# A two-layer decoder step with routed experts: the order of the shared expert's blocks, the count and the first gather

## The chip, the cores and the metric

The kernel runs on one core of a Trainium2 chip. A core has a matrix engine (PE, TensorE), a vector engine (DVE), a scalar engine (ACT), a general engine (POOL), and SP, which here only issues transfers. All transfers run on 16 DMA engines. Each engine works through its own instructions in order, and they meet only at semaphores. The metric is the device time of one execution in microseconds, lower is better.

## The reference

320 tokens (256 of a prompt, 8 x 8 of samples) of width 1024 pass two layers in float32. Layer 0 mixes tokens by sliding-window attention, layer 1 by gated linear attention. Each is followed by a mixture of experts, which is the part that the change touches:

```python
scores = sigmoid(x @ router_w); sel = scores + router_b
# 4 of 8 groups by their two best scores, then the 8 best experts of 64 for each token
w = w / sum(w) * 2.5
routed[t] = sum over the 8 experts e of t:  w[t, e] * (silu(x_t @ wg[e]) * (x_t @ wu[e])) @ wd[e]
shared    = (silu(x @ swg) * (x @ swu)) @ swd
out       = routed + shared          # SHARED_FF = EXPERT_FF = 256
```

Each of the 64 experts has 3 MB of weights in a layer (three matrices of 1024 x 256), and all of them are read, so that the two layers read some 400 MB for the experts alone.

## The kernel before, in words

`moe(l)` has a head, in which the experts are sorted by how many tokens chose them, and then 29 passes. Rank 0 is the expert with the most tokens, and every rank has a fixed number of slots (96, 64 or 32; what doesn't fit is done by `rest` behind the passes). A pass (`PASSES`) does two or three ranks at a time, 128 slots in all: pass 0 the ranks 0 and 56, pass 1 the ranks 1 and 57, pass 2 three ranks. Up to four passes make a batch (`BATCHES` = 2, 4, 4, ...), whose tokens are gathered together.

Weights come through two rings. `gu_ring` has five slots of 2 MB for gate and up weights, `dn_ring` five of 1 MB for down weights. SP issues the gate and up weights of all experts in the order of the passes (`expert_stream`), and those of down for the first five; it begins when the order is known (`order_full`), and ahead of each expert it waits until PE is through with the slot (`last_item`). ACT issues the other down weights. Two of the five slots of `gu_ring` first hold the shared expert's weights: gate and up in one, down in the other. They are given free by `item_used.up(pe.drain())`, once behind the shared expert's last block of gate and up, once behind the shared down product; the fourth and the fifth expert go into them.

The head, on PE: router logits; transposes of the tokens into rows (`token_rows`); the shared expert's gate and up products in four blocks `shared_up(f, u, ks)` of eight chunks `ks` each, with the steps of the sorting set between them. These steps are the count (how many tokens chose each expert, ten small bf16 matmuls from L1615 to L1626, which need the top-8 mask of DVE, `topk_full`, and the rows copied by ACT, `tok_hi`), the sort (L1629 and L1630, a permutation matrix that DVE forms from the count), the transposes of the weights (L1634) and the positions (L1640). DVE (from L1669) forms mask, permutation, order, weights, positions and parts of weights in turn; it also forms the shared expert's hidden values, a product with what ACT's SiLU gives (`ovh`, `sh_h`). POOL forms the low halves of the token rows (`tok_lo`) once the order is known.

Then, in the second block of code, on PE: the shared down product (L1842) into the banks that sum the output; `fill(0, f)` for f = 0 to 3 (L1808), which gathers the tokens of the first batch by matmuls with the selection `sel` that DVE forms (`select(0)`, L1990), while ACT (L1922) and DVE (L1998) copy the gathered tokens out; `slot_weights(0)` (L1818), the weight of each slot, which ACT copies out and forms (L1927 to L1935). After that the passes: gate and up (L1869), the gather for the next batch, transposes (L1890), the scatter of the pass before (`combine`, L1830 and L1833), down (L1908).

Of the kernel before, what the change touches and what calls it, by code (L numbers as in the profile page):

```python
# [24 lines left out]
ALU = mybir.AluOpType  # L25
# [5 lines left out]
KC = D // P  # L31
# [3 lines left out]
T = SEQ + NS  # L35
# [26 lines left out]
def places(experts):  # L62

    out, o = [], 0
    for r, cap in experts:
        out.append((r, cap, o))
        o += cap
    return out
# [18 lines left out]
NB = len(BATCHES)  # L87
NFILL = 4 + 8 * (NB - 1)
# [143 lines left out]
def decoder_step(nc, a, debug=None):  # L232
    with ExitStack() as ctx:
        names = {}

        def sb(name, shape, dt=F32, c=ctx):
            names[name] = names.get(name, -1) + 1
            return c.enter_context(nc.sbuf_tensor(f"s_{name}_{names[name]}", shape, dt))

        def sem(name):  # L240
            return ctx.enter_context(nc.semaphore(name))
# [5 lines left out]
        bank = [pair[i // 2][:, i % 2, :] for i in range(4)]  # L247
# [21 lines left out]
        def cc(name):  # L269
            at, n = lay[name]  # L270
            part = next(p for p, (lo, hi) in const_range.items() if lo <= at < hi)
            lo = const_range[part][0]
            return csts[part][:, at - lo:at - lo + n]
# [1189 lines left out]
        S = {n: sem(n) for n in SEMS}  # L1463
# [55 lines left out]
        def moe(l):  # L1519
            with ExitStack() as c:  # L1520
# [8 lines left out]
                ovh = sb("ovh", [P, 2, T], c=c)  # L1529
# [4 lines left out]
                def step(ins):  # L1534
                    settled(nc.vector, ins)

                with ExitStack() as c1:
# [30 lines left out]
                    def _(pe):  # L1568
# [32 lines left out]
                        def shared_up(f, u, ks):  # L1601

                            for k in ks:
                                last = pe.matmul(bank[2 + 2 * f + u][:, 0:T], shw[:, k, FF * u + P * f:FF * u + P * f + P], hT[:, k, :],  # L1604
                                                 start=(k == 0), stop=(k == KC - 1))
                            return last

                        slot_in[sg_].wait(pe, sg_n)
                        shared_up(0, 0, range(KC))
                        pe.wait_ge(S["tok_hi"], 6 * l + 6)  # L1610
                        pe.wait_ge(S["topk_full"], l + 1)
                        pe.wait_ge(A["mod_full"], mod_at(19 + 4 * l))
# [11 lines left out]
                        pe.matmul(W1[:, 128:192], ones_b, m0, start=True, stop=False)  # L1624
                        pe.matmul(W1[:, 128:192], ones_b, m1, start=False, stop=False)
                        pe.matmul(W1[:, 128:192], up2[0:NS, :], m2, start=False, stop=True).then_inc(S["cnt_psum"], 1)  # L1626
                        shared_up(0, 1, range(0, 2))
                        pe.wait_ge(S["perm_full"], l + 1)
                        pe.matmul(W0[0:1, 384:448], cc("ecol")[0:NE, :], perm[0:NE, :], start=True, stop=True)  # L1629
                        pe.matmul(W0[0:1, 448:512], cols[0:NE, 2:3], perm[0:NE, :], start=True, stop=True).then_inc(S["sort_psum"], 1)  # L1630
                        shared_up(0, 1, range(2, KC)).then_inc(S["sh_psum"], 1)
                        pe.wait_ge(S["pw_full"], l + 1)
                        for t in range(3):
                            last = pe.transpose(W1[:, t * P:(t + 1) * P], pw[:, t, :, :].rearrange("p u e -> p (u e)"), ident)  # L1634
# [34 lines left out]
                    def _(dve):  # L1669
# [63 lines left out]
                        step(dve.tensor_tensor(wovS[:, :, :], posS[:, :, :], cc("caprow").unsqueeze(1).to_broadcast([P, 3, NE]), ALU.subtract))  # L1733
                        step(dve.tensor_scalar(wovS[:, :, :], wovS[:, :, :], -BIG, None, ALU.is_ge))
                        step(dve.tensor_tensor(wovS[:, :, :], wovS[:, :, :], w_, ALU.mult))
                        dve.wait_ge(S["sh_silu"], 2 * l + 2)
                        dve.tensor_tensor(ovh[:, 1, :], ovh[:, 1, :], bank[5][:, 0:T], ALU.mult).then_inc(S["sh_h"], 1)

                c2 = ExitStack()
                sel = sb("sel", [P, 3, 4 * P], F32R, c=c2)  # L1740
# [59 lines left out]
                def _(pe):  # L1800
                    def fill(q, f):

                        b = (W1, W2)[f % 2]
                        width = P * BATCHES[q]
                        ms = (2 * f, 2 * f + 1) if q == 0 else (f,)
                        for x, m in enumerate(ms):
                            for n, (w, s) in enumerate(shown):
                                last = pe.matmul(b[:, width * x:width * x + width], w[:, m * P:(m + 1) * P], sel[:, s, 0:width],  # L1808
                                                 start=(n == 0), stop=(n == 4))
                        last.then_inc(S["fill_full"], 1)  # L1810

                    def slot_weights(q):

                        for j in range(BATCHES[q]):
                            ranks = [r for r, _ in PASSES[BATCH_START[q] + j]]
                            n4, at = 4 * len(ranks), 256 + 16 * j
                            for s in range(3):
                                last = pe.matmul(W0[:, at:at + n4].rearrange("p (e u) -> p e u", u=4), sel[:, s, P * j:P * j + P],  # L1818
                                                 wpartS[:, s, ranks[0]:ranks[-1] + 1:ranks[1] - ranks[0], :], start=(s == 0), stop=(s == 2))
                        return last  # L1820

                    def combine(p):
# [11 lines left out]
                                                 stop=(p == NP - 1 and y is ylo and half == 1))  # L1834
                        return last

                    slot_in[sd_].wait(pe, sd_n)
                    pe.wait_ge(S["sh_h"], 2 * (l + 1))
                    for t, (t0, tn) in enumerate(TILES):
# [2 lines left out]
                                last = pe.matmul(acc[(t, half)], ovh[:, f, t0:t0 + tn], shd[:, f, 512 * half:512 * half + 512],  # L1842
                                                 start=(f == 0), stop=False)
                    item_used.up(pe.drain())
                    pe.wait_ge(S["tok_lo"], 3 * (l + 1))
                    for f in range(4):
                        pe.wait_ge(S["sel_full"], l * NB + 1)
                        if f >= 2:
                            pe.wait_ge(S[("fill_act", "fill_dve")[f % 2]], l * NFILL // 2 + 1)
                        fill(0, f)  # L1850
                    slot_weights(0).then_inc(S["tr_full"], 1)

                    for p in range(NP):
                        if p == NP - 1:
# [3 lines left out]
                        if j == 0:  # L1858
                            f = 3 if q == 0 else 7
# [116 lines left out]
                @block.vector  # L1976
                def _(dve):
                    def select(q):

                        for h in range(BATCHES[q]):  # L1980
                            experts = PASSES[BATCH_START[q] + h]
                            caps = [cap for _, cap in experts]
                            if len(set(caps)) == 1:
                                n, cap, r0 = len(experts), caps[0], experts[0][0]
                                last = dve.tensor_tensor(sel[:, :, h * P:(h + 1) * P].rearrange("p t (e s) -> p t e s", s=cap),
                                                         cc("slot")[:, 0:cap].unsqueeze(1).unsqueeze(1).to_broadcast([P, 3, n, cap]),
                                                         posS[:, :, r0:r0 + n].unsqueeze(3).to_broadcast([P, 3, n, cap]), ALU.is_equal)
                            else:
                                for r, cap, o in places(experts):
                                    last = dve.tensor_tensor(sel[:, :, h * P + o:h * P + o + cap],  # L1990
                                                             cc("slot")[:, 0:cap].unsqueeze(1).to_broadcast([P, 3, cap]),
                                                             posS[:, :, r:r + 1].to_broadcast([P, 3, cap]), ALU.is_equal)
                        last.then_inc(S["sel_full"], 1)

                    def fill_out(q, f):

                        dve.wait_ge(S["fill_full"], filled(q, f))
                        dve.tensor_copy(fill_target(q, f), fill_source(q, f)).then_inc(S["fill_dve"], 1)  # L1998

                    dve.wait_ge(S["tok_lo"], 3 * (l + 1))  # L2000
                    select(0)
                    dve.wait_ge(S["h_kept"], 16 * (l + 1))
                    fill_out(0, 1)
                    fill_out(0, 3)
                    dve.wait_ge(S["tr_full"], l * (NP + 1) + 1)
                    select(1)
                    for p in range(NP):
                        if p == NP - 1:
                            left = any_left(dve)
                        q = BATCH_OF[p][0]  # L2010
                        dve.wait_ge(S["silu_full"], l * NP + p + 1)
                        dve.wait_ge(S["hT_full"], hT_at(p))
                        dve.scalar_tensor_tensor(hh[:, :], sg[:, :], wsl[p % 2][:, 0:1], W0[:, FF:2 * FF], ALU.mult, ALU.mult).then_inc(S["hh_full"], 1)  # L2013
                        for f in fills_in(p)[1::2]:
                            fill_out(q + 1, f)
                        for half in range(2):
                            dve.wait_ge(S["y_high"], 2 * (l * NP + p) + half + 1)
                            dve.tensor_tensor(ylo[:, half, :], (W1, W2)[half], yhi[:, half, :].bitcast(F32), ALU.subtract).then_inc(S["y_low"], 1)  # L2018
                            if half == 0:
                                dve.tensor_scalar(gt[:, :], cc("token"), wsl[p % 2][:, 1:2], None, ALU.is_equal).then_inc(S["gt_full"], 1)  # L2020
                        if last_of(p) and q + 2 < NB:
                            select(q + 2)
                    rest_dve(dve, left)
# [306 lines left out]
```

## Time and profile before

| | |
|---|---|
| median of 3 runs | 1546.19 us (1544.91 to 1547.66) |
| the profiled execution | 1550.64 us, its span 1548.5 us |
| mean granted TensorE clock | 0.979 |
| PE busy | 1461.7 us, 94% |
| DVE, ACT busy | 27%, 25% |
| DMA | 509.64 MB, mean 329 GB/s |

The profile is of one execution; times in it count from the start of its span. A busy share is an average over stages with different limits. Ends of matmuls are modelled. The chain of waits is the work that ended last, followed back from step to step; a stretch that it names "issue" is time in which the engine waited for nothing that the profile shows. The experts of layer 0 run from about 280 to 758 us, those of layer 1 from about 1040 to 1521 us.

### The profile page before, as it was taken

Reading aid. Unit: us, or ns where it says so; the run is one execution under the profiler, and the core shown is the slowest. Engines: PE = TensorE matmul, PEld = TensorE weight load, DVE = VectorE, ACT = ScalarE, POOL = GpSimd, SP = SyncE. Lnnn points to the kernel's source line nnn. Section 1 sums busy time; section 2 is a strip of 40 time slices with the busy share of each in tenths; the row PEclk is TensorE's granted clock in tenths of the full one; section 3 lists DMA queues with packets and bytes.
Section 4 is the critical chain, followed back from the end, with each engine's and each line's share of the span. In section 5 each row is a group of like instructions: output and inputs, shape, how many; then the busy total and the mean of one; then the engine's idle time right before and its main releaser. Section 6 shows DMA issues by size and latency. Waiting matters only on the chain.

```text
span 1548.5 us, 21530 instructions
## 1 busy us (share of the span) xinstructions
PE 1461.7 (94%) x8438; PEld 745.5 (48%) x8438; DVE 411.5 (27%) x998; ACT 383.4 (25%) x1089; POOL 49.9 (3%) x86
## 2 busy tenths in 40 slices
PE   6998999999999999999999989999999999999896
PEld 2344655544444444544465445554444544545444
DVE  2126524222121212211353142432121221211113
ACT  3024313222221212211363122412222221221113
POOL 0000301000000000000100010010000000000000
PEclk9998999999999999999999998999999999999998
DMA  9987506999999999999851252198999999999981
GB/s 395 395 326 287 201 28 249 395 361 421 420 421 420 421 421 422 420 420 421 330 218 55 109 204 91 53 371 336 407 420 420 421 421 421 422 421 421 411 335 35
DMA packets 65894, 509.64 MB, mean 329 GB/s; under 512 B 7776, under 2 KB 8048, under 8 KB 10208
## 3 DMA queue, kind: packets, MB, share of 16 engines
q1 hardware_dynamic: 45072, 366.43, 57.5%
q10 hardware_dynamic: 16992, 123.74, 19.4%
q0 software_dynamic: 3728, 18.07, 3.2%
q8 instruction: 69, 1.13, 0.3%
q14 instruction: 33, 0.27, 0.0%
HBM read 499.16 MB, written 11.01 MB: 329 GB/s over the span
## 4 chain that ended last, share of the span: by engine, by line
PE 79%; DMA 13%; ACT 3%; DVE 2%; issue 1%; SPq 1%; ACTq 0%; DVEq 0%
PE bank L1869 24%; PE banks L1908 11%; DMA s_gu_ring<-in_moe_wu_dram 10%; PE banks L1808 7%; PE banks L431 5%; PE banks L1066 4%; PE ybank L1830 3%; PE banks L1830 3%; PE bank L1833 3%; PE banks L679 2%; PE bank L498 2%; PE banks L1094 2%; DMA s_gu_ring<-in_wqkv_dram 2%; DMA s_gu_ring<-in_ada_w_dram 2%; PE banks L1604 1%
## 5 line engine op out<-in xcount | busy, mean ns | idle before, releaser
L1869 PE MATMUL bank<-s_gu_ring,s_hbuf 128*32 128x512 f32 (+1 forms) x2752 | 415.0, 602 | 18.1 <-DMA s_gu_ring<-in_moe_wu_dram 14.1
L1869 PEld LDWEIGHTS bank<-s_gu_ring,s_hbuf 128*32 128x32 f32 (+1 forms) x2752 | 130.2, 121 | 293.7 <-issue 293.7
L1908 PE MATMUL banks<-s_dn_ring,s_hTs 128*32 128x512 f32 (+1 forms) x1376 | 211.5, 596 | 7.1 <-ACT s_hTs L1958 5.2
L2018 DVE TENSOR_TENSOR s_ylo<-banks,s_yhi 128x512 fp32r<-128x512 f32 x116 | 80.2, 691 | 328.9 <-ACT s_yhi L1966 328.9
L1808 PE MATMUL banks<-s_sel,s_htok 128*128 128x512 f32 (+2 forms) x640 | 149.4, 381 | 0.5 <-issue 0.5
L1808 PEld LDWEIGHTS banks<-s_sel,s_htok 128*128 128x128 f32 x640 | 109.8, 188 | 61.6 <-issue 45.2
L1966 ACT CAST s_yhi<-banks 128x512 fp32r<-128x512 f32 x116 | 67.9, 586 | 268.8 <-PE banks L1908 268.8
L2013 DVE SCALAR_TENSOR_TENSOR s_hh<-s_sg,s_wsl,bank 128x256 f32<-128x256 f32 x58 | 27.9, 480 | 348.4 <-ACT s_sg L1950 348.4
L1908 PEld LDWEIGHTS banks<-s_dn_ring,s_hTs 128*32 128x32 f32 (+1 forms) x1376 | 58.4, 119 | 128.1 <-issue 120.9
L1950 ACT ACTIVATE s_sg<-bank 128x256 f32<-128x256 f32 x58 | 22.3, 384 | 389.2 <-PE bank L1869 389.2
L1998 DVE COPY s_hbuf<-banks 128x512 f32<-128x512 f32 (+1 forms) x60 | 40.4, 673 | 119.0 <-PE banks L1808 119.0
L1066 PE MATMUL banks<-s_gu_ring,s_hbuf 128*128 128x512 f32 x128 | 55.9, 593 | 0.5 <-DVE s_rs L1350 0.5
L1922 ACT COPY s_hbuf<-banks 128x512 f32<-128x512 f32 (+1 forms) x60 | 34.3, 572 | 80.7 <-PE banks L1808 80.7
L1934 ACT ACTIVATE s_wsl<-s_rstd 32x1 f32<-32x1 f32 (+1 forms) x172 | 50.2, 292 | 3.0
L679 PE MATMUL banks<-s_gu_ring,s_hbuf 128*128 128x512 f32 x96 | 44.4, 617 | 3.4 <-DMA s_gu_ring<-in_wqkv_dram 3.4
L1830 PE MATMUL ybank<-s_yhi,s_gt 128*128 128x512 f32 x116 | 41.3, 437 | 0.0
L431 PE MATMUL banks<-s_qk,s_gu_ring 128*128 128x320 f32 x128 | 38.0, 461 | 0.8 <-ACT s_qk L1287 0.8
L1066 PEld LDWEIGHTS banks<-s_gu_ring,s_hbuf 128*128 128x128 f32 x128 | 24.2, 191 | 29.1 <-issue 28.2
L431 PE MATMUL banks<-s_hbuf,s_gu_ring 128*128 128x320 f32 x128 | 36.8, 450 | 0.9 <-DVE s_hbuf L974 0.9
L1830 PE MATMUL banks<-s_yhi,s_gt 128*128 128x512 f32 x116 | 36.3, 394 | 0.0
L1830 PE MATMUL ybank<-s_ylo,s_gt 128*128 128x512 f32 x116 | 36.1, 392 | 0.0
L1830 PE MATMUL banks<-s_ylo,s_gt 128*128 128x512 f32 x116 | 36.0, 392 | 0.0
(409 smaller groups left out, 1489.6 us busy)
## 6 DMA issues: line engine op xcount, KB each, us to landing
s_gu_ring<-in_moe_wg_dram SPq DMA_DIRECT2D x128, 1024.0 KB, 14.6
s_gu_ring<-in_moe_wu_dram SPq DMA_DIRECT2D x128, 1024.0 KB, 19.9
s_dn_ring<-in_moe_wd_dram ACTq DMA_DIRECT2D x118, 1024.0 KB, 12.8
s_gu_ring<-in_ada_w_dram SPq DMA_DIRECT2D x24, 2048.0 KB, 12.2
s_gu_ring<-in_win_dram SPq DMA_DIRECT2D x6, 2048.0 KB, 12.1
s_dn_ring<-in_moe_wd_dram SPq DMA_DIRECT2D x10, 1024.0 KB, 17.1
s_gu_ring<-in_wqkv_dram SPq DMA_DIRECT2D x3, 2048.0 KB, 25.6
s_gu_ring<-in_wo_dram SPq DMA_DIRECT2D x2, 2048.0 KB, 8.4
```

The costliest lines, as they stand in the source:

```text
L431: last = pe.matmul(b[:, 0:T], item(slot)[:, k, (m % 4) * P:(m % 4 + 1) * P], src[:, k, :], start=(k == 0), stop=(k == KC - 1))
L679: last = pe.matmul(b[:, :], hT[:, k, t0:t0 + P], item(slots[cch])[:, k, :], start=(k == 0), stop=(k == KC - 1))
L1066: last = pe.matmul(b[:, :], hT[:, k, t0:t0 + P], w[:, k, :], start=(k == 0), stop=(k == KC - 1))
L1808: last = pe.matmul(b[:, width * x:width * x + width], w[:, m * P:(m + 1) * P], sel[:, s, 0:width], start=(n == 0), stop=(n == 4))
L1830: pe.matmul(acc[(t, half)], g[:, t * P:(t + 1) * P], y[:, half, :], start=False, stop=(p == NP - 1 and y is ylo))
L1833: last = pe.matmul(bank[6][:, :], g[:, 320 - 64 * half:448 - 64 * half], y[:, half, :], start=False, stop=(p == NP - 1 and y is ylo and ha ...
L1869: last = pe.matmul(W0[o:o + n, :], tokens_of(p, k)[:, o:o + n], w[:, k, :, :], start=(k == 0), stop=(k == KC - 1))
L1908: last = pe.matmul((W1, W2)[half][o:o + n, :], hTs[:, f, o:o + n], dn_ring[:, dn_of[(l, r)][0], w0:w0 + 512], start=(f == 0), stop=(f == 1))
L1934: act.activation(wsl[p % 2][o:o + n, 0:1], w[:, 0:1], ACT.Identity, bias=w[:, 1:2])
L1966: act.copy(yhi[:, half, :], (W1, W2)[half]).then_inc(S["y_high"], 1)
L1998: dve.tensor_copy(fill_target(q, f), fill_source(q, f)).then_inc(S["fill_dve"], 1)
L2018: dve.tensor_tensor(ylo[:, half, :], (W1, W2)[half], yhi[:, half, :].bitcast(F32), ALU.subtract).then_inc(S["y_low"], 1)
```

## The change

Two things are put in another order, and nothing is added or left out. In the head, the first block of the shared expert is cut: its chunks 0 to 3 stay ahead of the count, 4 and 5 come between count and sort, 6 and 7 and the whole second block behind the sort (before: the whole first block ahead of the count, two chunks of the second between, six behind). In the second part, the gather for the first batch and its slot weights come ahead of the shared down product that frees the slot. On DVE the product of the shared expert's second half moves from the end of the first part to behind the first selection.

```diff
--- before.py
+++ after.py
@@ -1606,7 +1606,7 @@
                             return last
 
                         slot_in[sg_].wait(pe, sg_n)
-                        shared_up(0, 0, range(KC))
+                        shared_up(0, 0, range(4))
                         pe.wait_ge(S["tok_hi"], 6 * l + 6)
                         pe.wait_ge(S["topk_full"], l + 1)
                         pe.wait_ge(A["mod_full"], mod_at(19 + 4 * l))
@@ -1624,11 +1624,12 @@
                         pe.matmul(W1[:, 128:192], ones_b, m0, start=True, stop=False)
                         pe.matmul(W1[:, 128:192], ones_b, m1, start=False, stop=False)
                         pe.matmul(W1[:, 128:192], up2[0:NS, :], m2, start=False, stop=True).then_inc(S["cnt_psum"], 1)
-                        shared_up(0, 1, range(0, 2))
+                        shared_up(0, 0, range(4, 6))
                         pe.wait_ge(S["perm_full"], l + 1)
                         pe.matmul(W0[0:1, 384:448], cc("ecol")[0:NE, :], perm[0:NE, :], start=True, stop=True)
                         pe.matmul(W0[0:1, 448:512], cols[0:NE, 2:3], perm[0:NE, :], start=True, stop=True).then_inc(S["sort_psum"], 1)
-                        shared_up(0, 1, range(2, KC)).then_inc(S["sh_psum"], 1)
+                        shared_up(0, 0, range(6, KC))
+                        shared_up(0, 1, range(KC)).then_inc(S["sh_psum"], 1)
                         pe.wait_ge(S["pw_full"], l + 1)
                         for t in range(3):
                             last = pe.transpose(W1[:, t * P:(t + 1) * P], pw[:, t, :, :].rearrange("p u e -> p (u e)"), ident)
@@ -1733,8 +1734,6 @@
                         step(dve.tensor_tensor(wovS[:, :, :], posS[:, :, :], cc("caprow").unsqueeze(1).to_broadcast([P, 3, NE]), ALU.subtract))
                         step(dve.tensor_scalar(wovS[:, :, :], wovS[:, :, :], -BIG, None, ALU.is_ge))
                         step(dve.tensor_tensor(wovS[:, :, :], wovS[:, :, :], w_, ALU.mult))
-                        dve.wait_ge(S["sh_silu"], 2 * l + 2)
-                        dve.tensor_tensor(ovh[:, 1, :], ovh[:, 1, :], bank[5][:, 0:T], ALU.mult).then_inc(S["sh_h"], 1)
 
                 c2 = ExitStack()
                 sel = sb("sel", [P, 3, 4 * P], F32R, c=c2)
@@ -1834,6 +1833,13 @@
                                                  stop=(p == NP - 1 and y is ylo and half == 1))
                         return last
 
+                    pe.wait_ge(S["tok_lo"], 3 * (l + 1))
+                    for f in range(4):
+                        pe.wait_ge(S["sel_full"], l * NB + 1)
+                        if f >= 2:
+                            pe.wait_ge(S[("fill_act", "fill_dve")[f % 2]], l * NFILL // 2 + 1)
+                        fill(0, f)
+                    slot_weights(0).then_inc(S["tr_full"], 1)
                     slot_in[sd_].wait(pe, sd_n)
                     pe.wait_ge(S["sh_h"], 2 * (l + 1))
                     for t, (t0, tn) in enumerate(TILES):
@@ -1842,13 +1848,6 @@
                                 last = pe.matmul(acc[(t, half)], ovh[:, f, t0:t0 + tn], shd[:, f, 512 * half:512 * half + 512],
                                                  start=(f == 0), stop=False)
                     item_used.up(pe.drain())
-                    pe.wait_ge(S["tok_lo"], 3 * (l + 1))
-                    for f in range(4):
-                        pe.wait_ge(S["sel_full"], l * NB + 1)
-                        if f >= 2:
-                            pe.wait_ge(S[("fill_act", "fill_dve")[f % 2]], l * NFILL // 2 + 1)
-                        fill(0, f)
-                    slot_weights(0).then_inc(S["tr_full"], 1)
 
                     for p in range(NP):
                         if p == NP - 1:
@@ -1999,6 +1998,8 @@
 
                     dve.wait_ge(S["tok_lo"], 3 * (l + 1))
                     select(0)
+                    dve.wait_ge(S["sh_silu"], 2 * l + 2)
+                    dve.tensor_tensor(ovh[:, 1, :], ovh[:, 1, :], bank[5][:, 0:T], ALU.mult).then_inc(S["sh_h"], 1)
                     dve.wait_ge(S["h_kept"], 16 * (l + 1))
                     fill_out(0, 1)
                     fill_out(0, 3)
```

## Rows read from the trace of the kernel before

**Rows 1.** The page: busy time; DMA by slice of 38.7 us; the chain's lines.

```profile
PE 1461.7 (94%) x8438; PEld 745.5 (48%) x8438; DVE 411.5 (27%) x998; ACT 383.4 (25%) x1089; POOL 49.9 (3%) x86
...
DMA  9987506999999999999851252198999999999981
...
PE bank L1869 24%; PE banks L1908 11%; DMA s_gu_ring<-in_moe_wu_dram 10%; PE banks L1808 7%; PE banks L431 5%; PE banks L1066 4%; PE ybank L1830 3%; PE banks L1830 3%; PE bank L1833 3%; PE banks L679 2%; PE bank L498 2%; PE banks L1094 2%; DMA s_gu_ring<-in_wqkv_dram 2%; DMA s_gu_ring<-in_ada_w_dram 2%; PE banks L1604 1%
```

**Rows 2.** Busy by stretch: stretch, length, each engine, PEclk, DMA share, GB/s.

```profile
340.00:355.00 15.00, 15.00 (x116) 7.18 (x116) 2.91 (x5) 4.00 (x13) 0.00 (x0) 1.00 1.01 423
```

**Rows 3.** Instructions in time, PE: start, length, what, [idle before <- what ended it].

```profile
681.94 8.41 PE L1869 MATMUL bank<-s_gu_ring,s_hbuf 128*32 128x512 f32 x64 [3.29 <-DMA s_gu_ring<-in_moe_wu_dram]
...
1443.52 9.91 PE L1869 MATMUL bank<-s_gu_ring,s_hbuf 128*32 128x512 f32 x64 [4.33 <-DMA s_gu_ring<-in_moe_wu_dram]
```

**Rows 4.** Busy by stretch, first transfers and behind the second pass.

```profile
250.00:252.50 2.50, 2.50 (x13) 1.73 (x12) 2.24 (x5) 0.43 (x2) 2.50 (x2) 1.00 0.63 187
...
315.00:317.00 2.00, 2.00 (x25) 0.69 (x20) 0.46 (x1) 0.59 (x1) 0.00 (x0) 1.00 0.49 205
317.00:319.00 2.00, 2.00 (x24) 0.73 (x20) 1.34 (x4) 0.58 (x1) 0.00 (x0) 1.00 0.08 29
```

**Rows 5.** Chain of waits, layer 0, 230 to 300 us: start, length, what.

```profile
241.90 4.31 PE banks L1604 x16
...
247.02 1.27 PE banks L1604 x4
...
257.49 4.52 PE ybank L1604 x16
...
263.21 3.67 PE ybank L1842 x8
266.88 3.43 PE banks L1842 x8
270.31 1.87 PE bank L1842 x8
...
272.44 5.05 PE banks L1808 x40
...
280.04 7.07 PE bank L1869 x64
```

**Rows 6.** Instructions in time, layer 0, what the steps of the head need.

```profile
242.45 0.65 ACT L1660 CAST s_htok<-banks 64x512 fp32r<-64x512 f32 x1
...
242.77 0.63 DVE L1697 TENSOR_TENSOR s_mb<-s_mm,s_slc 128x192 bf16<-128x192 f32 x2
...
254.22 2.34 POOL L1563 TENSOR_TENSOR s_htok<-s_hbuf,s_htok 64x1024 fp32r<-64x1024 f32 x1 [0.50 <-POOL s_htok L1563]
...
260.29 0.35 DVE L1735 TENSOR_TENSOR s_wovS<-s_wovS,banks 128x192 f32<-128x192 f32 x1
...
262.03 0.44 ACT L1666 ACTIVATE s_ovh<-ybank 128x320 f32<-128x320 f32 x1 [9.15 <-PE ybank L1604]
...
262.98 1.16 DVE L1990 TENSOR_TENSOR s_sel<-s_cst,s_posS 128x288 fp32r<-128x288 f32 x4
...
277.31 0.73 PE L1818 MATMUL bank<-s_wpartS,s_sel 128*128 128x8 f32 x6
...
279.65 0.17 ACT L1935 COPY s_wsl<-s_rstd 32x1 f32<-32x1 f32 x1
```

**Rows 7.** Layer 1: slot weights in time; the first pass in the chain.

```profile
1037.29 0.73 PE L1818 MATMUL bank<-s_wpartS,s_sel 128*128 128x8 f32 x6
...
1040.01 8.58 PE bank L1869 x64
```

**Rows 8.** Issues of SP in time: the first and the fifth expert's gate weights.

```profile
249.83 0.35 SPq L1496 DMA_DIRECT2D s_gu_ring<-in_moe_wg_dram  x1
...
272.80 0.35 SPq L1496 DMA_DIRECT2D s_gu_ring<-in_moe_wg_dram  x1
```

**Rows 9.** Busy by stretch, layer 1, start of the first pass.

```profile
1040.00:1042.50 2.50, 2.49 (x12) 0.67 (x16) 0.39 (x2) 0.00 (x0) 0.00 (x0) 0.50 0.98 403
```

## Prediction

> **What bounds the kernel now.** I read the page's shares first, then the busy time by stretches, then the chain of waits around the routing and the head of the experts, then the instructions in order of time there. The page shows TensorE (PE) busy for 94% of the span and the DMA slices at 9 for nearly all of both expert stages [rows 1]. Two resources are thus close to their limit, and the question is which of them sets the time of an expert stage, and from where on. By stretches [rows 2] the 16 DMA engines move some 421 GB/s from 340 us on (the row shown is the first of 27 of 15 us up to 745, of which none is under 416), and transfers of gate and up weights hold 10% of the chain [rows 1]; the last of them in each layer end PE's waits at 681.94 and 1443.52 us, and from there PE runs to the end of the layer without them [rows 3]. Before that, however, the engines stand nearly still: their share is 0.49 and 0.08 between 315 and 319 us [rows 4]. In that hole nothing is queued; it ends when PE has finished work and so freed buffers. So every transfer after the hole goes out at a time that PE sets, and the late transfers are requests of the same uninterrupted queue. I conclude that the head of the experts, up to the third pass, is PE's, and that whatever PE gains there moves the rest of the layer, transfers included, by the same amount.
>
> In the head the chain [rows 5] is PE without a gap from 241.90 to 262.01 us: first shared block, count, the second block in two pieces, transposes, the other two blocks. Then come two holes. PE waits 1.20 us (262.01 to 263.21) for SiLU and the product on DVE, before the shared down product. And after the gather (to 277.49) and the slot weights, first pass at 280.04: the slot weights start at 277.31 and last 0.73, so PE stands from 278.04 to 280.04, 2.00 us, for ACT, which copies the weights out and forms the slots, last at 279.65 + 0.17 [rows 6]. The second layer repeats the pattern: its second hole runs from 1037.29 + 0.73 = 1038.02 to 1040.01 [rows 7].
>
> **Part 1, half a block of the shared expert ahead of the count.** Four of the eight chunks of a block now follow the count instead of preceding it. A block of eight takes 4.31 us [rows 5], so the count can start 2.15 us earlier, at 244.06. What it waits for is ready: the top-8 mask ends at 242.77 + 0.63 = 243.40, the last rounded token row at 242.45 + 0.65 = 243.10 [rows 6]; 0.6 us is left. DVE's permutation and the sort follow with the same two chunks between, also 2.15 us earlier, and with them the order of the experts, the DMA issues of SP and POOL's subtractions. PE itself gains nothing: the same chunks are only in another order, the number of switches is the same, and there was no idle time to remove between 241.90 and 262.01. Between sort and transposes ten chunks stand now instead of six, so PE comes there at the same time as before, while DVE's weights move forward with the count. Cost on the path: 0. What moves is the first expert's transfer: issue 249.83 becomes 247.68 [rows 8]. The share of 0.63 in 250.0 to 252.5 [rows 4] puts the first data at 250.93, 1.1 us after the issue; it becomes 248.78. But the first pass needs only two experts, and 3 x 1.049 MB at 423 GB/s [rows 2] are 7.44 us for one: they are there by 265.8 before, 263.7 after, and are wanted at 277. Gain bounded by 0 and 2.15 us a layer (the whole advance, were the transfers the bound); I take 0.
>
> **Part 2, gather and slot weights ahead of the shared down product.** It uses both holes. After 262.01 PE needs the first selection. On DVE this now comes ahead of the shared product: it starts where that began to wait, at 260.29 + 0.35 = 260.64, takes 1.16 and is ready at 261.8 [rows 6]. POOL's last subtraction ended at 254.22 + 2.34 = 256.56 [rows 6] and comes 2.15 us earlier. So PE goes on after a drain; the same drain cost 0.26 ahead of the gather (270.31 + 1.87 = 272.18 to 272.44) [rows 5]. Then: 262.01 + 0.26 + gather 5.05 + slot weights 0.55 (277.49 to 278.04) = 267.87; shared down 3.67 + 3.43 + 1.87 = 8.97 = 276.84; drain 0.25 = 277.09 for the first pass, against 280.04. **2.95 us a layer.** What covers the moved waits: ACT's slots (1.8 us after the slot weights) and the last DVE copy lie beside 8.97 us of shared down, with 7 us to spare. DVE's shared product waits for the SiLU, which ends at 262.03 + 0.44 = 262.47 [rows 6]; 0.5 us later it is done, and is wanted at 267.9. Queued behind it on DVE are the gather's copies, the first of them wanted 2.5 us after the gather starts, at 264.8, so they lose nothing. ACT has its SiLU ahead of its first copy, which is wanted at 263.5. Within the gather the third and fourth block wait for copies of the first two as before, and stood for nothing there. Should the selection or the block edge be late, the cost is bounded by the old hole of 1.20 us; should the drain turn out free, 0.26 is gained. I take 2.95, with 2.0 and 3.2 as ends (3.2 is the sum of both holes).
>
> **The slot that comes free later.** The buffer of the shared down weights is freed by the drain behind that product, and the fifth expert goes into it. SP issued it at 272.80, 0.62 after PE's end at 272.18 [rows 5, 8]. Now it is 276.84 + 0.62 = 277.5, 4.7 us later, with first data 1.1 us after that, 278.6. Four experts last until 248.78 + 4 x 7.44 = 278.54. So the engines pause by 0.1 us at most, and the fifth expert is complete at 286.0 (288.1 before). Next is the sixth, issued after the first pass: 277.09 + 7.07 + 0.2 = 284.4, ahead of that. The third pass, which uses the fifth expert, starts at 314.6. Cost: 0. The Trainium skill ("DMA: Bandwidth & Descriptors", Anatomy of one DMA) gives about 2.0 us of fixed cost for one DMA; by that figure the pause would be near 1 us and still ends before PE has use for the data. The trace's issue-to-data of 1.1 us is shorter, since it leaves out the completion.
>
> **The clock.** In layer 1 the granted clock falls to 0.50 (1.2 GHz) in 1040.0 to 1042.5, right behind the hole of 2.00 us and the tiny slot-weight matmuls [rows 9], and the first pass takes 8.58 us instead of 7.07 [rows 5, 7]. In layer 0 the same hole costs nothing: 7.07. So the hole's removal is worth 0 or 1.51 us a layer beyond its length. The Trainium skill ("TensorE: Matmul & The Clock Gate", What's actually happening) says that the slow state is the default and activity lifts it; by that rule the dense shared down ahead of the first pass keeps the clock up. Since the timed runs lie 4.45 us below the profiled one, I can't tell how often they pay this; I take 0.3 us for both layers, ends 0 and 3.0.
>
> **The sum.** Two layers x 2.95 = 5.9. Against the profiled execution, 1550.64 us (span 1548.5 and 2.1 around it), with its own slow first pass gone: 1550.64 - 5.9 - 1.5 = 1543.2. The median of the runs is 1546.19: 1546.19 - 5.9 - 0.3 = **1540.0 us**. Ends by the terms: 1546.19 - 4.0 = 1542.2 and 1546.19 - 6.4 - 3.0 = 1536.8.
>
> **Rivals.** (1) The stream is the bound from its start. For it: the DMA slices at 9 right behind the start [rows 1]. Then a layer gains what the fifth expert gains, 2.1 us: 1542.0. Against it: the hole at 315 to 319.
>
> (2) The gain is swallowed by the late waits. PE waited 3.29 and 4.33 us for transfers at 681.94 and 1443.52 [rows 3]; if the stream doesn't move, these grow by 2.95 and nothing is left: 1546.2. For it: their 10% of the chain; against it the same hole.
>
> (3) Slower: as (2), and the longer waits cost the clock. After those two waits the first pass took 8.41 and 9.91 us instead of 7.07, and behind them the layer is PE's to its end, so this is paid. A pass wholly at 1.2 GHz takes 14.1: at most 5.7 + 4.2 = 9.9 us, half of it as an estimate, 5.0: 1551.2. It decides as soon as the stream moves by less than PE; if both move together the waits keep their length, which speaks against it.
>
> **Chances.** Forecast 0.78, (1) 0.08, (2) 0.09, (3) 0.05. A measurement of this kernel can tell 0.2%, 3.1 us, from no change, so faster means below 1543.1: 0.82 (the forecast but for 0.01 of it, and most of (1)); same 0.13; slower 0.05. The forecast's own range is 1537 to 1543; to hold 8 in 10 with the clock's share on either side I give 1536.5 to 1544.
>
> **What would show it.** Right: count at 244.1 with no wait ahead of it; PE going from the last shared block into the gather within 0.3 us; first pass some 3 us earlier in relation to the first shared block, at clock 1.0; the hole in the transfers still there behind the second pass; late waits of PE as long as before; both layers shorter by 3 us. Wrong: PE waiting ahead of the gather for the selection, a stall within it, the hole gone, or late waits longer by what the head gained. The forecast falls if the time is above 1543.1.

## The result and the profile after

| | before | after |
|---|---|---|
| median of 5 runs | 1546.19 us (1544.91 to 1551.18) | 1539.40 us (1537.76 to 1541.54) |
| profiled execution, span | 1550.64, 1548.5 us | 1539.78, 1537.8 us |
| mean granted TensorE clock | 0.979 | 0.981 |

The medians lie 6.8 us apart. The ratio of the two kernels' runs is 0.9949, 7.9 us less, with an interval of 0.9932 to 0.9967, that is 5.1 to 10.5 us less. Forecast were 1540.0 us, in 1536.5 to 1544.

The page of the changed kernel, the lines that answer to [rows 1]:

```profile
PE 1456.9 (95%) x8438; PEld 744.6 (48%) x8438; DVE 411.8 (27%) x998; ACT 383.3 (25%) x1089; POOL 49.7 (3%) x86
...
DMA  9987506999999999999851252198999999999981
...
PE bank L1868 24%; PE banks L1907 11%; DMA s_gu_ring<-in_moe_wu_dram 8%; PE banks L1807 8%; PE banks L431 5%; PE banks L1066 4%; PE ybank L1829 3%; PE banks L1829 3%; PE bank L1832 3%; PE banks L679 2%; PE banks L1094 2%; DMA s_gu_ring<-in_ada_w_dram 2%; PE bank L498 2%; DMA s_gu_ring<-in_wqkv_dram 1%; PE banks L1604 1%
```

Such a page hardly shows a change of 0.5%: the shares are nearly those of before, and the slices of the transfers are the same digit for digit. The chain of waits in the head of layer 0 does (start, length, what), and answers to [rows 5]. Line numbers behind the change differ by one to six: the gather is L1807, the slot weights L1817, the shared down product L1848, gate and up of a pass L1868.

```profile
240.18 2.15 PE banks L1604 x8
242.33 0.03 PE bank L1615
...
244.73 5.58 PE banks L1604 x20
...
259.15 1.18 DVE s_sel L1989 x4
260.32 0.21 issue
260.53 5.03 PE banks L1807 x40
265.56 0.57 PE bank L1817 x6
266.13 3.54 PE ybank L1848 x8
269.67 3.43 PE banks L1848 x8
273.10 1.88 PE bank L1848 x8
274.97 0.36 issue
275.34 7.07 PE bank L1868 x64
```

The first shared block is cut in two without a wait at the count. The selection is ready at 260.33 (259.15 + 1.18), the gather starts at 260.53, and nothing but 0.36 us behind the drain lies between the last of the shared down product and the first pass. From the first shared block to the first pass it is 275.34 - 240.18 = 35.16 us; before it was 280.04 - 241.90 = 38.14 [rows 5]. **The head is 2.98 us shorter, where 2.95 were forecast**, and in layer 1 it is the same: 1031.91 - 996.76 = 35.15, against 38.13. In that layer the first pass takes 7.07 us again, where before it took 8.58 [rows 7].

Beyond the head the spans of the two executions add up so: -1.72 us ahead of layer 0's head, -2.98 head, +0.36 passes of layer 0, -0.78 between the layers, -2.98 head, -2.60 from the first pass of layer 1 to the end; together -10.7. The parts other than the heads are of a size that differs from one execution to the next: in the run of part 1 alone, below, layer 0's head too begins 1.74 us earlier than in the kernel before (240.00 against 241.74), and nothing ahead of it was touched. The passes' own share is mostly the clock: of the +0.36, 0.33 is the slow pass behind layer 0's last wait for transfers (8.74 against 8.41), and of the -2.60, 1.51 is the first pass of layer 1 and 1.14 the pass behind its last wait (8.77 against 9.91). Hence the median, which moved by 6.8, is nearer to the two heads (5.96) than the span of the profiled pair is.

The late waits of PE, the last for transfers in each layer, are as long as before. In time order, the passes that answer to [rows 3]:

```profile
677.27 8.74 PE L1868 MATMUL bank<-s_gu_ring,s_hbuf 128*32 128x512 f32 x64 [2.99 <-DMA s_gu_ring<-in_moe_wu_dram]
...
1433.96 8.77 PE L1868 MATMUL bank<-s_gu_ring,s_hbuf 128*32 128x512 f32 x64 [4.29 <-DMA s_gu_ring<-in_moe_wu_dram]
```

2.99 and 4.29 us against 3.29 and 4.33: had the transfers stayed where they were, these would be 6.3 and 7.3. The transfers moved with PE's head. From the start of the first pass of layer 0 to the end of this wait it is 401.90 us before (681.94 - 280.04) and 401.93 after (677.27 - 275.34). In layer 1 it is 403.51 and 402.05; the 1.5 more before are the slow first pass, which came through in full.

### The profile page after: what moved, and what is told of

The parts are those of the page before. It is cut to its first block, busy times and chain, and to the rows that moved or that the text cites. A ratio compares the mean times of both kernels' runs of the same rounds, so it can differ in the third digit from the quotient of the medians.

```text
span 1537.8 us, 21530 instructions
## 1 busy us (share of the span) xinstructions
PE 1456.9 (95%) x8438; PEld 744.6 (48%) x8438; DVE 411.8 (27%) x998; ACT 383.3 (25%) x1089; POOL 49.7 (3%) x86
## 4 chain that ended last, share of the span: by engine, by line
PE 81%; DMA 11%; DVE 3%; ACT 3%; issue 1%; SPq 1%; ACTq 0%; DVEq 0%
PE bank L1868 24%; PE banks L1907 11%; DMA s_gu_ring<-in_moe_wu_dram 8%; PE banks L1807 8%; PE banks L431 5%; PE banks L1066 4%; PE ybank L1829 3%; PE banks L1829 3%; PE bank L1832 3%; PE banks L679 2%; PE banks L1094 2%; DMA s_gu_ring<-in_ada_w_dram 2%; PE bank L498 2%; DMA s_gu_ring<-in_wqkv_dram 1%; PE banks L1604 1%
## 5 line engine op out<-in xcount | busy, mean ns | idle before, releaser
L1868 PE MATMUL bank<-s_gu_ring,s_hbuf 128*32 128x512 f32 (+1 forms) x2752 | 414.3, 601 | 13.3 <-DMA s_gu_ring<-in_moe_wu_dram 12.6
L1868 PEld LDWEIGHTS bank<-s_gu_ring,s_hbuf 128*32 128x32 f32 (+1 forms) x2752 | 130.1, 120 | 289.9 <-issue 289.9
L1807 PE MATMUL banks<-s_sel,s_htok 128*128 128x512 f32 (+2 forms) x640 | 149.3, 381 | 0.5 <-DVE s_sel L1989 0.5
L1807 PEld LDWEIGHTS banks<-s_sel,s_htok 128*128 128x128 f32 x640 | 109.8, 188 | 60.8 <-issue 44.4
L1949 ACT ACTIVATE s_sg<-bank 128x256 f32<-128x256 f32 x58 | 22.3, 384 | 401.4 <-PE bank L1868 401.4
```

What stands on the lines that cost most here:

```text
L1868: last = pe.matmul(W0[o:o + n, :], tokens_of(p, k)[:, o:o + n], w[:, k, :, :], start=(k == 0), stop=(k == KC - 1))
```

## The experiments

The experiments ran in three sets, each on another chip: e1 to e4, e5 to e8, e9 to e12. Runs of the kernel before had a median of 1546.19 us in the first, 1545.63 in the second and 1545.82 in the third. Of these, only the first has the changed kernel (e3). So differences against it are taken from the ratios to the kernel before, with e3 as the changed kernel's (0.9954), times 1546. "Head" is the time from the first matmul of the first shared block to the first of the first pass (38.3 us before, 35.3 after, by the instructions in order of time).

**e1, the first part alone.** The kernel before with

```diff
-                        shared_up(0, 0, range(KC))
+                        shared_up(0, 0, range(4))
...
-                        shared_up(0, 1, range(0, 2))
+                        shared_up(0, 0, range(4, 6))
...
-                        shared_up(0, 1, range(2, KC)).then_inc(S["sh_psum"], 1)
+                        shared_up(0, 0, range(6, KC))
+                        shared_up(0, 1, range(KC)).then_inc(S["sh_psum"], 1)
```

> Only the first part of the change: four chunks of the first shared block ahead of the count instead of eight. Theory (PE sets the head, the start of the transfers has slack): issue of the first expert 2.1 us earlier after the first shared block, first pass as late as before (38.1 us after the first shared block), time of before within 1 us, ratio 0.999 to 1.001. Rival (the stream is the bound from its start): 2.1 us less a layer, 1542, ratio 0.997.

Measured: 1547.22 us, ratio 1.0005 (0.9992 to 1.0019); heads 38.30 and 38.28 us, and both first passes slow, 8.52 and 8.77 us. The start of the transfers moves as it should. In the order of time:

```profile
240.00 2.32 PE L1604 MATMUL banks<-s_hbuf,s_gu_ring 128*128 128x320 f32 x8
...
245.94 0.35 SPq L1496 DMA_DIRECT2D s_gu_ring<-in_moe_wg_dram  x1
```

That is 5.94 us from the shared block to the first issue, against 8.09 before (241.74 to 249.83 [rows 8]): 2.15 us earlier, and worth nothing. The rival's ratio of 0.997 is outside the interval.

**e2, the second part alone.** The changed kernel with the three edits of e1 taken back.

> Only the second part: gather and slot weights ahead of the shared down product, and the product on DVE behind the first selection; the count as before. Theory: the whole gain, first pass 35.15 us after the first shared block, 1540, ratio 0.995 to 0.996. Rival (the parts help only together, since the fifth expert's transfer goes out 3 us later and needs the earlier start): a part of the 3 us a layer comes back as longer late waits, 1543 or more.

Measured: 1540.01 us, ratio 0.9960 (0.9946 to 0.9975); heads 35.33 and 35.33. The whole gain of the heads is here; the 0.9 us that the ratio of e3 is lower are within both intervals. The late waits were 4.24 and 4.02 us, no longer than the 4.29 us of the changed kernel; the parts don't need each other.

**e3, the changed kernel again.** No edit.

> The changed kernel once more, as the measure for this set: 1539.4 us, ratio 0.995. With the first result it says how far two measurements of one kernel lie apart.

Measured: 1538.95 us, ratio 0.9954 (0.9938 to 0.9970). Two measurements of one kernel lie 0.45 us apart.

**e4, the transfers start 3 us later.** The changed kernel with

```diff
                 sp.wait_ge(S["order_full"], l + 1)
+                sp.wait_ge(S["pw_full"], l + 1)
```

> The changed kernel, but SP starts the experts' transfers only when the token weights are formed as well, which is 2.9 us later than the order. Theory: the transfers pause for 4 us and more behind the second pass anyway, so the later start is taken from that pause and the time stays at that of the changed kernel (within 1 us); late waits of PE as long as before. Rival (the stream is the bound): 2.9 us more a layer, 1545.

Measured: 1540.04 us, ratio 0.9958 (0.9946 to 0.9971): 0.6 us above e3, with intervals that cover each other; heads 35.32 and 35.36. The first issue comes 8.91 us behind the start of the shared block (5.95 in the changed kernel), so 3.0 us later. The rival's 1545 us, a ratio of 0.9992, is outside. Busy time by stretch shows where the 3 us went. First the changed kernel, then e4 (stretch, length, engines, PEclk, DMA share, GB/s):

```profile
300.00:305.00 5.00, 5.00 (x31) 4.36 (x30) 0.82 (x2) 1.82 (x5) 0.00 (x0) 1.00 0.91 331
305.00:310.00 5.00, 4.02 (x23) 2.71 (x25) 0.69 (x1) 1.33 (x8) 0.00 (x0) 1.00 1.00 419
310.00:315.00 5.00, 5.00 (x52) 1.89 (x48) 2.47 (x7) 1.17 (x2) 0.00 (x0) 1.00 0.54 180
```

```profile
300.00:305.00 5.00, 5.00 (x31) 4.38 (x30) 0.69 (x1) 2.00 (x6) 0.00 (x0) 1.00 1.01 423
305.00:310.00 5.00, 4.06 (x26) 2.66 (x28) 0.69 (x1) 1.15 (x7) 0.00 (x0) 1.00 1.01 421
310.00:315.00 5.00, 5.00 (x52) 1.80 (x48) 2.69 (x8) 1.17 (x2) 0.00 (x0) 1.00 0.74 267
```

The pause behind the second pass is shorter (0.54 became 0.74, and 0.91 became 1.01); the later start was taken from it. Summed over the stretches of 5 us from 295 to 335, the bytes fall short of a steady 423 GB/s by 6.9 us in the changed kernel and by 3.9 us in e4.

**e5, 11 us later.** The same line with `S["sort_psum"], 2 * l + 2`.

> The changed kernel, but SP starts the experts' transfers only when the positions are summed, some 10.8 us later than the order. Theory: the first pass still finds its two experts (landed by 273, wanted at 275); the pause of the stream behind the second pass, worth between 3.8 us by its share and 7 us by its bytes, is used up, and the rest, 4 to 7 us a layer, comes out as longer late waits: 1547 to 1553. Rival (PE's head alone sets the time, transfers never): 1539.4. Rival (the stream is the bound from its start): 10.8 us a layer, 1561.

Measured: 1546.91 us, ratio 1.0008 (0.9997 to 1.0019), 8.3 us above the changed kernel: 4.2 a layer, of 10.8 that the start was delayed. Both rivals, 1539.4 and 1561, are outside. The heads are still 35.33 and 35.31. The pause is gone (the same stretches as above, of e5):

```profile
300.00:305.00 5.00, 5.00 (x32) 3.80 (x24) 1.17 (x2) 1.55 (x3) 0.00 (x0) 1.00 1.00 413
305.00:310.00 5.00, 4.77 (x24) 3.72 (x24) 0.20 (x1) 1.98 (x10) 0.00 (x0) 1.00 1.02 426
310.00:315.00 5.00, 4.29 (x40) 1.47 (x44) 1.55 (x3) 1.17 (x2) 0.00 (x0) 1.00 1.02 423
```

From the first pass to the last late wait's end it is now 405.6 us in layer 0 (682.39 - 276.81) and 405.5 in layer 1, where it was 401.9 and 402.1. In one thing the expectation was off: the last waits are not longer (2.76 and 2.95 us). The loss comes as new, earlier waits, this one among them:

```profile
381.45 7.07 PE L1869 MATMUL bank<-s_gu_ring,s_hbuf 128*32 128x512 f32 x64 [2.01 <-DMA s_gu_ring<-in_moe_wu_dram]
```

So the start of the transfers has a slack between 3 and 11 us; 10.8 - 4.2 = 6.6 a layer, if what is beyond the slack comes through in full. It agrees with the 6.9 us that the pause was worth by its bytes.

**e6, the product ahead of the selection.** The changed kernel with DVE's order as before:

```diff
+                    dve.wait_ge(S["sh_silu"], 2 * l + 2)
+                    dve.tensor_tensor(ovh[:, 1, :], ovh[:, 1, :], bank[5][:, 0:T], ALU.mult).then_inc(S["sh_h"], 1)
                     dve.wait_ge(S["tok_lo"], 3 * (l + 1))
                     select(0)
-                    dve.wait_ge(S["sh_silu"], 2 * l + 2)
-                    dve.tensor_tensor(ovh[:, 1, :], ovh[:, 1, :], bank[5][:, 0:T], ALU.mult).then_inc(S["sh_h"], 1)
```

> The changed kernel, but DVE forms the shared expert's product ahead of the first selection, as before the change. Theory: PE then waits for the selection, which comes after SiLU (0.5), product (0.5) and selection (1.2): the gather starts 2.3 us after the last shared block instead of 0.2, so 2.1 us more a layer, 1543.6. Rival (the gather's place alone carries the gain): 1539.4.

Measured: 1545.30 us, ratio 0.9998 (0.9987 to 1.0009). The whole gain is gone, 6.8 us above the changed kernel, where 4.2 were expected. The instructions of the head in layer 0:

```profile
262.19 0.49 DVE L2000 TENSOR_TENSOR s_ovh<-s_ovh,ybank 128x320 f32<-128x320 f32 x1 [1.86 <-ACT s_ovh L1667]
...
262.59 1.16 DVE L1989 TENSOR_TENSOR s_sel<-s_cst,s_posS 128x288 fp32r<-128x288 f32 x4
...
263.89 6.52 PE L1807 MATMUL banks<-s_sel,s_htok 128*128 128x256 f32 x40 [2.21 <-DVE s_sel L1989]
```

The wait is 2.21 us, about as worked out. But the gather behind it takes 6.52 us instead of 5.03, and the stretch says why (PEclk, the granted clock, is the third number from the end):

```profile
262.50:265.00 2.50, 1.11 (x8) 1.14 (x9) 1.25 (x5) 0.00 (x0) 0.00 (x0) 0.92 1.01 423
265.00:267.50 2.50, 2.50 (x13) 2.50 (x13) 0.00 (x0) 0.58 (x1) 0.00 (x0) 0.50 1.01 419
267.50:270.00 2.50, 2.50 (x20) 2.50 (x20) 0.69 (x1) 0.59 (x1) 0.00 (x0) 0.89 1.01 419
```

The heads are 38.77 us in layer 0, with the fall of the clock, and 37.27 in layer 1, without it. The sum over both is 5.4 above the changed kernel's, of 6.8 measured; the other 1.4 are within the intervals.

**e7, needless work ahead of the first pass.** The changed kernel with twelve needless matmuls (`keep_awake(pe, b, n)` issues n of 128x128 into bank b):

```diff
                         pe.wait_ge(S["hT_full"], hT_at(p))
+                        if p == 0:
+                            keep_awake(pe, W0, 12)
```

> The changed kernel with twelve needless matmuls, 12 x 0.243 = 2.9 us, on PE right ahead of the first pass of each layer, all else as changed. Theory (whatever PE gains or loses in the head moves the rest of the layer): 5.8 us more, 1545.2, with late waits as long as before. Rival (the transfers take up the difference): late waits shorter by 2.9 us, time as changed, 1539.4.

Measured: 1544.88 us, ratio 0.9992 (0.9981 to 1.0004): 5.9 us above the changed kernel, 2.9 a layer; heads 38.07 and 38.05, 2.7 us longer each. The late waits are 3.14 and 3.24 us. Within the interval, what is added to the head comes through one to one; the rival's ratio of 0.9954 is outside.

**e8, the hole filled in the kernel before.** The kernel before with eight needless matmuls ahead of the first pass, between the wait for ACT's copies of the gather and that for DVE's:

```diff
                             pe.wait_ge(S["fill_act"], filled(q, f - 1) // 2 + 1)
+                            if p == 0:
+                                keep_awake(pe, W1, 8)
```

> The kernel before with eight needless matmuls (1.9 us) in the hole ahead of the first pass, so that PE is busy there and the first pass starts at the same time. Theory of the clock: the hole costs clock in a part of the executions, up to 1.5 us a layer; the time goes down by 0 to 3 us, the first pass takes 7.07 us in both layers. Rival (no clock in it): 1546.2 within 0.5.

Measured: 1544.66 us, ratio 0.9995 (0.9984 to 1.0006); heads 38.19 and 38.18, both first passes 7.07 us. That is 0.8 us less with an interval of 2.5 less to 0.9 more: not separable from nothing.

**e9, the wait of e6 filled.** e6 with

```diff
+                    pe.wait_ge(S["sh_h"], 2 * l + 1)
+                    keep_awake(pe, W0, 8)
                     pe.wait_ge(S["tok_lo"], 3 * (l + 1))
```

> As e6 (product on DVE ahead of the first selection), but PE fills its 2.2 us wait ahead of the gather with eight needless matmuls (1.9 us). e6 lost 7 us against the changed kernel where its longer head explains 3.9 (1.95 us a layer). Theory (the wait also costs clock: the gather took 6.52 us instead of 5.03 in one layer of e6's trace): the first pass 37.3 us after the first shared block in both layers, gather 5.03 us, and the time falls below that of e6 by up to 3 us: 1542 to 1544. Rival (the loss is something else): 1545.3 as e6.

Measured: 1542.48 us, ratio 0.9978 (0.9966 to 0.9990); heads 37.28 and 37.28. PE waits for the same selection and starts the gather at the same time, but it is 3.1 us faster than e6 by the ratios (their intervals just overlap). The gather takes 5.03 us in both layers. What is left, 3.7 us above the changed kernel, matches the 2 x 1.95 us of the longer head. So the rest of e6's loss is most likely the clock; its trace shows 1.49 us of it, in one layer.

**e10, the second pass's slots earlier.** The changed kernel, with ACT forming the slots of both passes of the first batch at once:

```diff
                     slot_out(0).then_inc(S["hT_full"], 1)
+                    slot_out(1)
...
-                        if p + 1 < NP and not last_of(p):
-                            if p:
-                                act.wait_ge(S["gt_full"], l * NP + p)
+                        if p and p + 1 < NP and not last_of(p):
+                            act.wait_ge(S["gt_full"], l * NP + p)
                             slot_out(p + 1)
```

> The changed kernel, with ACT forming the second pass's slots (four pairs of small instructions, 1.5 us) right behind those of the first, while PE does the shared down product, instead of within the first pass ahead of the copy that the down product waits for. Theory (the head up to the third pass is PE's, and gains there are kept): the second pass starts some 1.2 us earlier (PE stood 1.22 us there), 2.4 us less in all: 1537, ratio to before 0.9935. Rival (that wait is hidden by another, a copy of DVE): as changed, 1539.4.

Measured: 1538.49 us, ratio 0.9948 (0.9929 to 0.9966). Mostly the rival: ACT's copy starts 1.7 us earlier (11.23 us behind the start of the first pass, against 12.89), but the down product waits now for DVE's copy of the gather, which frees its bank:

```profile
285.94 0.38 ACT L1957 COPY s_hTs<-bank 128x256 f32<-128x256 f32 x1
286.84 0.69 DVE L1997 COPY s_hbuf<-banks 128x512 f32<-128x512 f32 x1 [1.84 <-PE banks L1807]
287.75 3.64 PE L1907 MATMUL banks<-s_dn_ring,s_hTs 128*32 128x512 f32 x32 [0.94 <-issue]
```

The profile names no releaser for the wait of 0.94 us; the code waits for that copy (`fill_dve`), which ends at 287.53, 0.22 us before. 0.94 us are left of 1.22, where the expectation had the wait gone, and the 0.3 a layer can't be told from none.

**e11, the late wait filled.** The changed kernel with `if p == 24: keep_awake(pe, W0, 12)` in the place of e7's edit; p = 24 is the last pass with three experts.

> The changed kernel with twelve needless matmuls (2.9 us) on PE in its wait ahead of the last pass with three experts, in each layer (waits of 3.0 to 4.3 us, behind which that pass took 8.7 us instead of 7.07). Theory: the wait's length is the transfers', but its cost in clock (1.7 us a layer) goes: 1536 to 1538, ratio to before 0.993 to 0.9945. Rival (where a wait is shorter than the filler, it lengthens it): 1539 or above.

Measured: 1538.57 us, ratio 0.9951 (0.9933 to 0.9970), the same as the changed kernel, and above the 1536 to 1538 expected. The pass behind the wait is at full clock again, and this is not worth its 1.7 us, because the stream takes it back three passes later. PE in e11:

```profile
674.28 2.94 PE L412 MATMUL bank<-s_cst 128*128 128x128 f32 x24
...
678.29 7.07 PE L1870 MATMUL bank<-s_gu_ring,s_hbuf 128*32 128x512 f32 x64 [1.06 <-DMA s_gu_ring<-in_moe_wu_dram]
...
725.87 7.09 PE L1870 MATMUL bank<-s_gu_ring,s_hbuf 128*64 128x512 f32 x32 [1.30 <-DMA s_gu_ring<-in_moe_wu_dram]
```

The pass at 725.87 is one that, in the changed kernel, starts without a wait for transfers:

```profile
725.04 7.04 PE L1868 MATMUL bank<-s_gu_ring,s_hbuf 128*64 128x512 f32 x32
```

From the last late wait's end that is 725.04 - 677.27 = 47.77 us there and 725.87 - 678.29 = 47.58 in e11. Layer 1 of e11 has such a new wait too, of 0.95 us; there 0.6 us are left (47.80 against 47.23).

**e12, both additions.** e10 and e11 together.

> The changed kernel with the additions of e10 and e11 together. Theory (they act in different places, one in PE's head, one behind the last late wait): the sum of both, 1534 to 1536, ratio to before 0.991 to 0.993. Rival (the earlier head only lengthens the late wait): as e11.

Measured: 1535.76 us, ratio 0.9947 (0.9928 to 0.9966), 7 runs from 1535.04 to 1541.60. The lowest median of all, within the 1534 to 1536 expected, but by its ratio, which was expected at 0.991 to 0.993, no better than the changed kernel. Nothing here beats it measurably.

## Why the prediction was right

- **PE's head bounds the start, and the rest follows it.** Shown from both sides: e7 makes the head 2.7 us longer and gets 2.9 a layer, within its interval the same; e4 delays the transfers by 3.0 us and gets nothing measurable. The late waits stayed at 3 to 4.4 us in both. From the start of the first pass to the end of the late wait it is 401.4 to 402.4 us in both layers of the kernel before, the changed one, e1 to e4 and e7, once what a slow first pass takes over 7.07 is taken off.
- **Part 1 at nothing.** Shown by e1 (0.8 us more, with an interval from 1.2 less to 2.9 more), though its mechanism worked to the hundredth: the first issue is 2.15 us earlier. The start it moves has some 6.6 us of slack anyway (e5).
- **Part 2 at 2.95 us a layer.** 2.98 measured in the trace, and e2 gives the gain alone. The terms: 0.26 us ahead of the gather (260.27 to 260.53; worked out 0.26), the gather 5.03 (5.05), slot weights 0.57 (0.55), shared down 8.85 (8.97), drain 0.36 (0.25). In one term the size was right and the reason was not. The prediction put the 0.26 us down to the drain and had the selection ready 0.2 us ahead of it. It is ready at 260.33, 0.06 after PE's last shared matmul, because DVE starts it 0.23 us after its last instruction, and it is what the profile names as ending the wait:

```profile
260.53 5.03 PE L1807 MATMUL banks<-s_sel,s_htok 128*128 128x256 f32 x40 [0.26 <-DVE s_sel L1989]
```

There is no slack left there: a microsecond of PE saved ahead of the gather would by this row only lengthen the wait.
- **DVE's product behind the selection.** The prediction counted this move as part of the sum without a price of its own. e6 gives it one: without it no gain can be measured. Of 6.8 us, 3.9 are the longer wait, and the rest is most likely clock (e9).
- **The fifth expert's slot.** SP issues it at 275.59, 0.62 us after the end of the shared down product at 274.97, as forecast; the stream has no pause there, its share is 1.02 from 275.0 to 277.5 and 1.01 from 277.5 to 280.0. Cost 0, as worked out.
- **The clock.** Forecast 0.3 us, with 0 to 3.0. The ratios of the changed kernel, 0.9949 and 0.9954, are 7.9 and 7.1 us, so 1 to 2 us more than the heads give, in intervals that also hold nothing. The traces speak for more as well: of the four heads with an open hole (before and e1) three have a slow first pass, 8.58, 8.52 and 8.77 us; of the 20 heads in the ten traces with the gather ahead (the changed kernel and all but e1, e7 and e8) the granted clock is 1.00 in the first pass of every one. But the timed comparison, e8, gives 0.8 us and can't tell it from 0. How often the clock falls in executions without a profile stays open.
- **Rival (3) had a wrong premise.** I wrote that behind the last late wait the layer is PE's to its end, so that a slow pass there is paid in full. e11 shows that the transfers are close behind for three passes more and take back most of 1.7 us. By this the rival's price, 1551.2, was probably too high; the forecast didn't rest on it.

## What to carry to other kernels

When an engine and a stream are both over 90% busy, look for the stream's first real pause: if the engine's own chain leads up to it, everything behind may shift with that chain. Here a microsecond there was worth a microsecond, while an earlier start of the stream was worth nothing; delaying either one on purpose, as in e7 and e4, tells which it is. If a wait of an engine is for a short chain elsewhere, put in front of it work that needs nothing from that chain, and check the order on the engine that has to deliver: the same move of matmuls gained some 7 us or nothing measurable, depending on which of two DVE operations came first. And what a slow clock costs depends on the place: behind the head it came through in full (1.5 to 1.7 us where the first pass was slow, before and e1), while behind the late wait the transfers took most of it back (e11).

## What the runs showed of the hardware

The granted clock fell to 0.50 behind waits as short as 2.0 us (with tiny matmuls in front) and 2.21 us (e6), and it did so in one layer and not in the other of the same execution. Tiny matmuls in front are not needed: in e7 PE waited 1.99 us for transfers behind a full down product, the clock is 0.50 from 529.5 to 532 us, and the pass took 8.77 us. Nor does the length of the wait decide alone: behind 2.34 us in the kernel before (531.56) and 2.76 us in e5 (682.39) the clock stayed at 1.00 and the pass at 7.07. One such fall made a pass of 7.07 us mostly 1.3 to 1.7 us longer, and up to 2.95 behind a wait of 4.27 (e4, 10.02 us). Where needless matmuls filled the wait it stayed up, in both layers of each of four kernels (e8, e9, e11, e12). The head itself is reproducible to 0.05 us (35.31 to 35.36 in the eight traces that have the changed kernel's), while whole executions of one kernel spread over 4 us and more. The longer ones have the lower mean clock: of 29 runs of the kernel before in the first set, the shortest took 1543.1 us at a mean granted clock of 0.986, the longest 1551.1 at 0.977.
